# Two matmuls instead of three for the value products and the 128-key scores of a dilated window attention

## The reference, cut to what matters

```python
scores = jnp.einsum("brnqhd,brnkhd->brnhqk", qb, kk).astype(jnp.float32) * (Dh ** -0.5) + bias
scores = jnp.where(mask[:, None], scores, -jnp.inf)
m = jnp.max(scores, axis=-1, keepdims=True)
p = jnp.exp(scores - m)
l = jnp.sum(p, axis=-1, keepdims=True)
o = jnp.einsum("brnhqk,brnkhd->brnqhd", p.astype(v.dtype), vv).astype(jnp.float32)
```

## Time and profile before

| | us |
|---|---|
| median of three runs | 1910.48 |
| lowest, highest | 1909.32, 1911.99 |
| the profiled execution | 1910.8 |
| its span, first to last instruction | 1909.0 |
| PE busy | 1879.7 |
| DVE busy | 1175.1 |
| ACT busy | 756.2 |
| POOL busy | 89.1 |
| mean granted TensorE clock, share of full | 0.998 |

### The profile page before, as it was taken

How to read it: one execution, slowest core, us unless ns; L and a number is a source line. 1 busy time by engine, 2 the same in 40 slices (tenths; PEclk the granted TensorE clock), 3 DMA queues, 4 the chain that set the end, 5 groups by cost and what they waited for, 6 DMA issues and landing times.

```text
span 1909.0 us, 23987 instructions
## 1 busy us (share of the span) xinstructions
PE 1879.7 (98%) x8981; PEld 1617.2 (85%) x8981; DVE 1175.1 (62%) x1582; ACT 756.2 (40%) x1390; POOL 89.1 (5%) x150
## 2 busy tenths in 40 slices
PE   6999999999999999999999999999999999999999
PEld 5788999999998888888888787877888888888887
DVE  5635643554343588898424626468878787877675
ACT  5423532353234146312702413265545454544443
POOL 1101110111010010000100000000000000000000
PEclk9999999999999999999999999999999999999999
DMA  7321322143213111012102604222222222257543
GB/s 252 140 93 66 134 90 93 51 138 117 88 51 119 53 45 45 14 53 66 37 31 57 188 23 154 78 78 67 72 94 72 93 74 91 66 194 275 166 142 100
DMA packets 133974, 184.18 MB, mean 96 GB/s; under 512 B 15929, under 2 KB 63033, under 8 KB 133881
## 3 DMA queue, kind: packets, MB, share of 16 engines
q1 hardware_dynamic: 125817, 172.33, 27.7%
q10 hardware_dynamic: 8064, 10.59, 1.5%
HBM read 142.92 MB, written 39.96 MB: 96 GB/s over the span
## 4 chain that ended last, share of the span: by engine, by line
PE 92%; DVE 4%; DMA 1%; ACT 1%; SPq 1%; issue 1%; POOL 0%; ACTq 0%; DVEq 0%
PE psum L240 29%; PE psum L242 29%; PE psum L241 29%; PE psum L495 1%; PE psum L970 1%; DMA grp<-group_out 1%; DVE wlo L198 1%; DMA x_rows<-in_x 1%; DVE grp L1449 0%; PE psum L351 0%; DVE acc L889 0%; DVE acc_odd L889 0%; ACT grp L1467 0%; PE psum L1725 0%; PE psum L920 0%
## 5 line engine op out<-in xcount | busy, mean ns | idle before, releaser
L240 PE MATMUL psum<-whi,act_lo 128*128 128x512 f32 x768 | 314.9, 410 | 2.3 <-DVE act_lo L1508 0.9
L242 PE MATMUL psum<-whi,act_hi 128*128 128x512 f32 x768 | 304.5, 396 | 0.0
L241 PE MATMUL psum<-wlo,act_hi 128*128 128x512 f32 x768 | 304.4, 396 | 0.0
L240 PEld LDWEIGHTS psum<-whi,act_lo 128*128 128x128 f32 x768 | 194.9, 254 | 17.4 <-issue 2.1
L242 PEld LDWEIGHTS psum<-whi,act_hi 128*128 128x128 f32 x768 | 195.1, 254 | 15.4
L241 PEld LDWEIGHTS psum<-wlo,act_hi 128*128 128x128 f32 x768 | 196.0, 255 | 13.2
L240 PE MATMUL psum<-act_hi,wlo 128*128 128x512 f32 x512 | 202.2, 395 | 0.0
L242 PE MATMUL psum<-act_hi,whi 128*128 128x512 f32 x512 | 199.6, 390 | 0.0
L241 PE MATMUL psum<-act_lo,whi 128*128 128x512 f32 x512 | 199.3, 389 | 0.0
L193 ACT CAST whi<-stage 128x512 fp32r<-128x512 f32 x200 | 120.4, 622 | 173.8 <-PE psum L242 165.6
L198 DVE TENSOR_TENSOR wlo<-stage,whi 128x512 fp32r<-128x512 f32 x200 | 129.0, 685 | 94.7 <-ACT whi L193 93.9
(11 more groups left out here) (247 smaller groups left out, 3587.4 us busy)
## 6 DMA issues: line engine op xcount, KB each, us to landing
stage<-in_w_in SPq DMA_DIRECT2D x144, 256.0 KB, 4.0
u_raw<-in_w_up SPq DMA_DIRECT2D x44, 512.0 KB, 5.0
stage<-in_w_down SPq DMA_DIRECT2D x44, 256.0 KB, 4.2
w_sums<-stage SPq DMA_DIRECT2D x44, 256.0 KB, 2.5
gated_scratch<-g_buf SPq DMA_DIRECT2D x22, 512.0 KB, 2.6
gated<-gated_scratch SPq DMA_DIRECT2D x44, 256.0 KB, 3.6
d_raw<-w_sums SPq DMA_DIRECT2D x44, 256.0 KB, 2.6
d_raw<-in_w_down SPq DMA_DIRECT2D x33, 256.0 KB, 3.4
```

The costliest lines, as they stand in the source:

```text
L240: nc.tensor.matmul(dst, lhs[1], rhs[0], start=first, stop=False, skip_group_check=True)
L241: nc.tensor.matmul(dst, lhs[0], rhs[1], start=False, stop=False, skip_group_check=True)
L242: return nc.tensor.matmul(dst, lhs[0], rhs[0], start=False, stop=last, skip_group_check=True)
```

## The change

The hi and lo halves of the keys and of the values are now halves of one tile (`k_both`, `v_both`), so that both can be given as one moving operand of 2 x 128 columns. A new helper `two` makes a product from a matmul of the stationary hi half by both moving halves, 256 columns wide (hi by hi goes into the first half of the output, hi by lo into the second), and one of the stationary lo half by the moving hi half, 128 columns, added to the first half of the output. The two halves of the output have to be added afterwards.

The value products of all Q tiles use it, and so do the scores of the narrow tiles. The scores of the wide tiles stay with `three`. The output of the value products is now twice as wide and takes two banks: heads 2 and 3 in bank 7, heads 0 and 1 in a low bank, which is bank 2 for groups 0 and 1 and bank 6 for group 2. ACT copies the first halves to `ob` by two instructions, and DVE adds the second halves to `ob` by two more, in iteration i for tile i-4, behind `pt_lo`. For narrow scores DVE adds the second halves and the bias first, waits for that, and then adds the first halves. `o_read` counts twice for each tile, for ACT's copy and for DVE's addition. Bank 2 is used by the norm transposes too, which brings new waits on PE: the norm transposes wait for the addition of tile i-5, and the value products in groups 0 and 1 wait for `hn_lo` of tile i-1. ACT's store waits for DVE's addition.

```diff
@@ -662,8 +662,9 @@
         off = FREE
-        kT = [at("k_hi", off, [NH, S], F32R), at("k_lo", off + 16384, [NH, S], F32R)]
-        vT = [at("v_hi", off + 32768, [NT, CW], F32R), at("v_lo", off + 49152, [NT, CW], F32R)]
+        k_both = at("k_both", off, [2, NH, S], F32R)
+        v_both = at("v_both", off + 32768, [2, NT, CW], F32R)
+        kT, vT = ([a[:, part] for part in range(2)] for a in (k_both, v_both))
         bact = [at("bact_hi", FREE, [FT, S], F32R), at("bact_lo", FREE + 16384, [FT, S], F32R)]
@@ -744,6 +745,11 @@
                 self.last = t == NT - 1
+                self.paired = kind == "Q"
+                self.low_bank = 6 if kind == "Q" and g == NG - 1 else 2
+                self.narrow = kind == "Q" and self.width == P
                 self.sq, self.qn, self.qT, self.sc, self.pt = (
@@ -753,6 +759,7 @@
         N_TILES = len(tiles)
+        NARROW = [tl.a for tl in tiles if tl.narrow]
         assert tiles[NT - 1].index == 2 * MT + NT - 1
@@ -773,10 +780,30 @@
         per_tile = 2 * 16
+        cmb_step = sem("cmb_step")
+        def pair_bank(tl, h):
+            return psum[:, tl.low_bank if h < 2 else 7, h % 2 * 2 * P:(h % 2 + 1) * 2 * P].rearrange(
+                "p (z d) -> p z d", z=2)
+        def pair_parts(tl):
+            halves = (psum[:, b, :].rearrange("p (h z d) -> p h z d", h=2, z=2) for b in (tl.low_bank, 7))
+            return [(half[:, :, 0, :], half[:, :, 1, :]) for half in halves]
+        def two(pe, dst, one, both, other, first, last):
+            nc.tensor.matmul(dst, one, both, start=first, stop=False, skip_group_check=True)
+            return nc.tensor.matmul(dst[:, 0, :], other, both[:, 0, :], start=False, stop=last, skip_group_check=True)
         heads_scores = banks(3).rearrange("p (h c) -> p h c", h=NH)
...
             return bact[part][:, :, t * P:(t + 1) * P]
+        def pair_dst(tl):
+            return ob[:, tl.t % 2, :].rearrange("p (h d) -> p h d", h=NH)
         def bank_channels(b):
@@ -933,6 +960,9 @@
                         pe.wait_ge(sig_done, FT)
+                    earlier = tile_of(part, i - 5, "QX")
+                    if earlier and earlier.paired:
+                        pe.wait_ge(o_read, 2 * earlier.a + 2)
                     norm_pe(pe, tl.n, tl.index, tl.qn)
@@ -953,8 +983,13 @@
                     for h in range(NH):
-                        mm = three(pe, banks(3)[:, h * 256:h * 256 + tl.width], (tl.qT[0][:, h, :], tl.qT[1][:, h, :]),
-                                   (keys[0][:, h, :], keys[1][:, h, :]), True, True)
+                        dst = banks(3)[:, h * 2 * P:(h + 1) * 2 * P]
+                        if tl.narrow:
+                            mm = two(pe, dst.rearrange("p (z d) -> p z d", z=2), tl.qT[0][:, h, :],
+                                     k_both[:, :, h, c0:c0 + P], tl.qT[1][:, h, :], True, True)
+                        else:
+                            mm = three(pe, dst[:, 0:tl.width], (tl.qT[0][:, h, :], tl.qT[1][:, h, :]),
+                                       (keys[0][:, h, :], keys[1][:, h, :]), True, True)
                     mm.then_inc(s_done, 1)
@@ -972,15 +1007,22 @@
                     pe.wait_ge(pt_lo_done, tl.a + 1)
-                    if tl.kind == "Q" or tl.t == 0:
-                        if tl.a >= 1:
-                            pe.wait_ge(o_read, tl.a)
-                    else:
+                    if tl.kind == "X" and tl.t:
                         pe.wait_ge(b_lo, tl.t)
+                    elif tl.a >= 1:
+                        pe.wait_ge(o_read, 2 * tl.a)
+                    if tl.paired and tl.low_bank == 2:
+                        pe.wait_ge(hn_lo, max(other.n for other in tiles[:i] if other.kind != "V") + 1)
                     for h in range(NH):
...
                             probs = [half[:, c:c + P] for half in tl.pt]
+                            ends = j == 0, j == tl.width // P - 1
+                            if tl.paired:
+                                dst = pair_bank(tl, h)
+                                mm = two(pe, dst, probs[0], v_both[:, :, tl.t - tl.prev + j, h * HD:(h + 1) * HD],
+                                         probs[1], *ends)
+                                continue
                             if tl.kind == "Q":
@@ -988,8 +1030,7 @@
                                 lhs, rhs = vals, probs
-                            mm = three(pe, psum[:, 7, h * HD:(h + 1) * HD], lhs, rhs, j == 0,
-                                       j == tl.width // P - 1)
+                            mm = three(pe, psum[:, 7, h * HD:(h + 1) * HD], lhs, rhs, *ends)
                     mm.then_inc(o_done, 1)
@@ -1047,7 +1088,7 @@
                 if tl:
-                    act.wait_ge(o_read, tl.a + 1)
+                    act.wait_ge(o_read, 2 * tl.a + 2)
                     dst = rows_of(tl)
@@ -1057,12 +1098,14 @@
                         act.wait_ge(o_stored[tl.a % 2], per_tile * (tl.a // 2))
-                    nc.scalar.copy(ob[:, tl.t % 2, :], psum[:, 7, :]).then_inc(o_read, 1)
+                    for b, (main, _) in enumerate(pair_parts(tl)):
+                        copied = nc.scalar.copy(pair_dst(tl)[:, 2 * b:2 * b + 2, :], main)
+                    copied.then_inc(o_read, 1)
                 tl = tile_of(part, i - 4, "X")
                 if tl:
-                    act.wait_ge(o_done, tl.a + 1)
                     if tl.t == 0:
                         act.wait_ge(prod_done, FT)
+                    act.wait_ge(o_done, tl.a + 1)
                     nc.scalar.copy(bact_tile(0, tl.t), bank_channels(7)).then_inc(b_hi, 1)
@@ -1110,8 +1153,13 @@
                         src = tl.sc[:, :, 0:tl.width]
-                        nc.vector.tensor_tensor(src, heads_scores[:, :, 0:tl.width], bias[:, :, 2 * P - tl.width:],
-                                                ALU.add).then_inc(s_read, 1)
+                        more = bias[:, :, 2 * P - tl.width:]
+                        if tl.narrow:
+                            nc.vector.tensor_tensor(src, heads_scores[:, :, P:2 * P], more, ALU.add).then_inc(cmb_step, 1)
+                            dve.wait_ge(cmb_step, NARROW.index(tl.a) + 1)
+                            more = src
+                        nc.vector.tensor_tensor(src, heads_scores[:, :, 0:tl.width], more, ALU.add).then_inc(s_read, 1)
                         dve.wait_ge(s_read, tl.a + 1)
@@ -1129,11 +1177,19 @@
                                             ALU.subtract).then_inc(pt_lo_done, 1)
+                tl = tile_of(part, i - 4, "Q")
+                if tl:
+                    dve.wait_ge(o_read, 2 * tl.a + 1)
+                    for b, (_, cross) in enumerate(pair_parts(tl)):
+                        dst = pair_dst(tl)[:, 2 * b:2 * b + 2, :]
+                        total = nc.vector.tensor_tensor(dst, cross, dst, ALU.add)
+                    total.then_inc(o_read, 1)
                 free_time()
...
                     dve.wait_ge(b_hi, tl.t + 1)
-                    nc.vector.tensor_tensor(bact_tile(1, tl.t), bank_channels(7), bact_tile(0, tl.t).bitcast(F32),
+                    nc.vector.tensor_tensor(bact_tile(1, tl.t), bank_channels(7),
+                                            bact_tile(0, tl.t).bitcast(F32),
                                             ALU.subtract).then_inc(b_lo, 1)
@@ -1228,7 +1284,7 @@
                 gate_features(pe, 0, glu_slots, start=2)
-                pe.wait_ge(o_read, A_Q)
+                pe.wait_ge(o_read, 2 * A_Q)
                 pe.wait_ge(pt_lo_done, A_Q)
@@ -1322,7 +1378,6 @@
         cmb_exp = sem("cmb_exp")
-        cmb_step = sem("cmb_step")
         cmb_done = sem("cmb_done")
@@ -1412,7 +1467,7 @@
                 ins.then_inc(cmb_step, 1)
-                dve.wait_ge(cmb_step, n)
+                dve.wait_ge(cmb_step, len(NARROW) + n)
             def each(a):
```

## The result

The changed kernel takes 1923.86 us (median of 4 runs, 1921.04 to 1926.39) against 1911.1 us for the kernel before on the same chips: a ratio of 1.0068, 95% interval 1.005 to 1.0085. It is slower by some 13 us, outside what could be taken for no change.

The account below looks back on a forecast made before the run. PE, busy 98% of the span, was taken as the bound: -20.7 + 19.8 + 1.5 + 1.0 + 0.8 + 2.8 = +5.2 us, +6.2 with 1 us for neglected items, +15.5 with the clock: 1926.0 us, range 1915 to 1932.

Parts of the forecast that it names:

- The rival that columns count: Narrow scores and value products: a pair takes as long as a triple, PE saves nothing; 28 us slower, 1939; chance 0.04.
- What PE saves: Scores of 13 narrow tiles and value products of all 24 Q tiles: two matmuls for three save PE 20.7 us.
- The first wait: Value products in groups 0 and 1 wait until ACT and DVE have read bank 2: together 19.8 us.
- slow restarts: PE's first matmuls behind each of 14 waits ahead of value products run slowly: about 0.1 each, 1.5 us.
- the faster rival: ACT and DVE get ahead while PE waits, gaps fall to their floor: -6.3 us, no clock fall, 1904.2; chance 0.05.
- The second wait: Norm transposes wait for DVE's addition of tile i-5: 0.8 us in the first wide tile, 2.8 at group 2's end.
- It costs nothing more in groups 0 and 1: After the first wide tile, the norm transposes' wait for additions adds nothing there, since both cycles have the same length.
- a fall for each of the three, 3 x 3.1 = 9.3 us: Two waits at the weight splits and one ending group 2 each halve the clock: 9.3 us; ends none and 15.5.
- the trace holds one longer wait of a warm PE: Kernel before, 2.79 us ahead of the matmul at 33.77: clock 0.50 from 33.1 to 39.9 us, 3.1 us lost.
- The sum: Whole kernel: +5.2 us at full clock, +6.2 with 1 us for neglected items, +15.5 with the clock, so 1926.0 us.
- the 1 us for what I had left at nothing: Allowance for the 128-wide matmul behind a 256-wide one and the pre-add's wait on its own result: 1 us.
- the clock holds: Rival: the clock falls stay out, so 1916.7 us, or 1919.8 with one of them; chance 0.27.

Follow-up runs that it names:

- Scores alone: Changed kernel with only the narrow scores by two matmuls, all value products by three: 1906.33 us, ratio 0.9976 against the kernel before.
- copies and additions early: Changed kernel with ACT's copy moved ahead of the exponentials and DVE's additions ahead of the probabilities' split: 1918.07 us, ratio 1.0029 against the kernel before.
- heads first: Changed kernel with value products of heads 2 and 3 first, the bank 2 wait only ahead of heads 0 and 1: 1914.9 us, ratio 1.0015.
- chosen tiles: Both edits, narrow scores by two, value products by two only in group 2 and seven wide tiles: 1897.89 us, ratio 0.9929 against the kernel before.
- both edits: Changed kernel with value products of heads 2 and 3 first, and ACT's copy and DVE's additions moved early: 1907.65 us, ratio 0.9974.
- filling them: Changed kernel with 22 useless 256-wide matmuls put into each of PE's three longest waits: 1921.85 us, ratio 1.005 against the kernel before.

## Why the prediction was right, point by point

I forecast 1926.0 in a range of 1915 to 1932; measured were 1923.86. The mechanism holds: PE saves what the spacings said, two new waits of PE take more than that back, and the clock falls behind the long ones.

- **The pairs.** Computed 0.232 us, measured 0.23. The rival that columns count is refuted: 384 columns took 0.34 us in three pieces and 0.23 in two. The rule of the Trainium skill, page "TensorE: Matmul & The Clock Gate", section "Back-to-back issue gap", cited in the prediction, has them equal for isolated matmuls; the same section says that this rule counts too little for 128 columns in a stream in which each matmul has a weight load. This is such a stream, and the trace (0.113 us where the rule has 0.056) bears the section out in that, though not in its figure for such a stream, which is 0.081. The two parts of the moving operand, 16 KB apart, cost nothing extra that shows.
- **What PE saves.** 20.7 us was computed from the spacings; by the spacings of the changed kernel it is 20.3. Scores alone gave 5.3 of 5.7 at full clock.
- **The first wait.** Predicted 14 waits with 20.8 us (19.8 from the rows and 1.0 for the narrow tiles) and 1.5 for slow restarts, 22.3 together; measured 14 with 19.9 listed and 3.4 beside the list, 23.3. The restarts were right in size for another reason: behind the wait at 206.18 the next matmul stands 0.19 us away instead of 0.17, so hardly anything is lost there. What is lost is that the value matmuls no longer start before the last transpose has ended. That the gaps between existing instructions could be read off as waits held because the late engine hangs on PE's own scores and can't get ahead; the faster rival fell on that. The two long ones came out longer than read (3.06 and 3.39 listed, where 2.78 and 2.71 were read), and with copies and additions early they didn't: the prediction gave the new work behind `pt_lo` no effect on the splits. The two experiments on this wait (heads first, chosen tiles) move it by the amounts computed from the same rows.
- **ACT and DVE.** Two copies were put at 0.65 us and two additions at 0.75; they took 0.63 and 0.75.
- **The second wait.** Predicted 0.8 and 2.8; measured 0.6 and 3.25, at the two places named. "It costs nothing more in groups 0 and 1" holds only since the first wait covers it: with heads 2 and 3 first, it came out in four places in group 0.
- **The clock: right in kind, wrong in size.** The step "a fall for each of the three, 3 x 3.1 = 9.3 us" gave 9.3 where the runs show nearly 6. In the profile each of the three has its fall, but two of them lasted 3.4 us and one 6.8, where the one known row showed 6.8, and the three lost 6.2 us together. And the early fall of the kernel before is itself not there in each run: the profile of the changed kernel has none at that place, behind a wait of 2.69 us, while the ten others have one of 3.4 or 6.8 us. The sentence that the trace holds one longer wait of a warm PE is wrong: there is a second one, of 2.54 us at 1294.34, and it passed at full clock. Read beside the first, it would have said before the result that a wait of this size may or may not make the clock fall. The step that no row spoke for, waits of 1.5 to 1.9 us, has its answer: they make the clock fall in some executions. And in one profile, that of both edits, even two waits, of 0.73 us and then of 0.92 us within 2 us, had a fall behind them (a line of the timeline, then the stretch):

```profile
1176.39 0.47 PE L240 MATMUL psum<-whi,act_lo 128*128 128x512 f32 x1 [0.92 <-DVE act_lo L1563]
```

```profile
1176.74:1180.15 3.41, 3.41 (x10) 2.63 (x9) 0.69 (x1) 0.00 (x0) 0.00 (x0) 0.50 0.99 357
```

- **The sum.** At full clock +6.2 was forecast, and 6.1 measured over the runs (7.1 in the Q tiles of the profiles). That it meets so closely is partly luck: the saving was 0.4 us smaller and the waits 1.5 us longer than their terms, the 1 us for what I had left at nothing stood in for half of that, and the measured 6.1 is itself good to 1 or 2 us. The rival "the clock holds" named the same sum without the falls, which the runs do have.

What is open: how much of the nearly 6 us belongs to which wait. I tried only the three longest, and filling them moved the falls to others. Why an idle time makes the clock fall in one execution and not in another is open too.

## What to carry to other kernels

When an output moves into a bank that another step uses, list who drains that bank, and read the wait straight off the old timeline: the end of the last reader less the start of the new writer, for each iteration, the ones with extra work (here the weight splits) apart. If PE is the bound, order the work inside the step so that what doesn't need the bank comes first (here two of four heads, 0.93 us, which cover most of a 0.94 us wait), and drain it where the helpers idle, not behind their longest chain. And use the cheaper form only in those tiles in which it is cheaper than its wait: leaving it out of nine tiles of 24 took another 9.8 us off the version with both edits (1907.65 to 1897.89), 5.8 of them at full clock and the rest in falls of the clock that stayed out.

## What the runs showed of the hardware that I had not expected

- The granted clock falls to 0.50 (1.2 GHz) behind waits of PE as short as 1.51 and 1.72 us, in one execution and not in another of nearly the same kernel, and once behind two of 0.73 and 0.92 us; the stretches were 3.41 or 6.83 us long. PE loses half of what it is busy in them, so in this kernel a wait of PE costs up to 1.7 us beyond its own length behind a short one and up to 3.4 behind a long one. Long ones were seen only with waits of 2.69 us or more.
- A wait that the profile lists is counted from the modelled end of the matmul before it. In a stream in which the next matmul starts before that end, PE stood still for 0.24 us more than listed at each of the 14 waits ahead of value products.
- In a pair, the 128-wide matmul starts 0.17 us after the 256-wide one (0.19 behind a wait) and the next 256-wide one 0.06 us after that; in a uniform stream 128-wide ones stood 0.113 apart and 256-wide ones 0.118. The sum of the pair is what the two uniform streams give (0.23), but its parts aren't.
